# The first mixer's attention: transposes of 64-row halves, both heads in one bank

## What is computed

```python
s = jnp.einsum('nbqgrd,nbkgd->nbgrqk', qb, kw) * dh ** -0.5
p, denom, m = masked_softmax(s + bias, mask)
o = jnp.einsum('nbgrqk,nbkgd->nbqgrd', p, vw) / denom
...
o = g[..., 0:1] * o_cmp + g[..., 1:2] * o_sel + g[..., 2:3] * o_win
```

## Time and profile before

| | us |
|---|---|
| median of three runs | 1298.45 (1298.41 to 1301.5) |
| the profiled execution | 1297.85 |
| its span, first to last instruction | 1296.1 |
| the stage of the change, first turning to the output projection's first matmul | 95.27 to 141.29 |
| TensorE, VectorE, ScalarE busy in the span | 98 %, 63 %, 50 % |

### The profile page before, as it was taken

The page is one execution under the profiler, slowest core; times in us unless marked ns, Lnnn a source line. Parts: engine busy times, 40 slices in busy tenths (PEclk is TensorE's granted clock), DMA queues, the critical chain, the costliest instruction groups (busy, mean ns, idle before and its releaser), DMA issues.

```text
span 1296.1 us, 19580 instructions
## 1 busy us (share of the span) xinstructions
PE 1266.3 (98%) x7427; PEld 1058.7 (82%) x7427; DVE 812.3 (63%) x1194; ACT 641.7 (50%) x932; POOL 275.7 (21%) x362
## 2 busy tenths in 40 slices
PE   9999999999999999999999999999999999999997
PEld 7986788888799987888888788888887778888886
DVE  4568665555574476654656755656789876755554
ACT  4439554444453365543444644445544683534442
POOL 6520210000000041103000589602276210200000
PEclk9999999999999999999999999999999999999999
DMA  9960655555455645467655555654545346555651
GB/s 303 268 130 20 179 163 194 193 182 182 155 195 183 175 116 161 166 194 175 215 189 163 189 181 185 224 194 135 191 130 163 130 130 195 191 184 193 194 189 38
DMA packets 155996, 224.79 MB, mean 173 GB/s; under 512 B 13507, under 2 KB 108091, under 8 KB 155932
## 3 DMA queue, kind: packets, MB, share of 16 engines
q1 hardware_dynamic: 145248, 212.55, 51.7%
q0 software_dynamic: 10064, 10.54, 4.2%
q10 hardware_dynamic: 620, 0.83, 0.2%
HBM read 222.56 MB, written 1.25 MB: 173 GB/s over the span
## 4 chain that ended last, share of the span: by engine, by line
PE 82%; DVE 8%; ACT 4%; POOL 2%; DMA 2%; issue 2%; DVEq 0%; SPq 0%; POOLq 0%; ACTq 0%
PE bank L223 24%; PE bank L225 23%; PE bank L224 23%; PE bank L244 5%; DVE units_lo L178 2%; PE bank L232 2%; PE bank L747 1%; DMA raw_units<-in_ffn_w_up 1%; ACT arena L1584 1%; PE bank L1000 1%; DVE arena L3092 1%; PE bank L239 1%; POOL rows L1261 1%; DVE arena L3083 1%; DVE arena L2545 1%
## 5 line engine op out<-in xcount | busy, mean ns | idle before, releaser
L666 DVE TENSOR_TENSOR units_lo<-raw_units,units_hi 128x2048 fp32r<-128x2048 f32 x96 | 223.0, 2322 | 154.3 <-ACT units_hi L620 154.3
L223 PE MATMUL bank<-units_hi,turned_hi 128*128 128x512 f32 (+1 forms) x792 | 307.1, 388 | 3.0 <-DVE units_lo L178 1.3
L225 PE MATMUL bank<-units_hi,turned_lo 128*128 128x512 f32 (+1 forms) x792 | 302.1, 381 | 0.0
L224 PE MATMUL bank<-units_lo,turned_hi 128*128 128x512 f32 (+1 forms) x792 | 301.7, 381 | 0.0
L178 DVE TENSOR_TENSOR units_lo<-raw_units,units_hi 128x2048 fp32r<-128x2048 f32 (+2 forms) x101 | 228.3, 2268 | 96.0 <-ACT units_hi L170 95.6
L170 ACT ACTIVATE units_hi<-raw_units 128x2048 fp32r<-128x2048 f32 (+2 forms) x101 | 189.5, 1885 | 100.2 <-PE bank L225 76.8
L620 ACT ACTIVATE units_hi<-raw_units 128x2048 fp32r<-128x2048 f32 x96 | 183.5, 1911 | 103.9 <-PE bank L225 95.6
L223 PE MATMUL bank<-units_hi,second_hi 128*128 128x512 f32 (+1 forms) x560 | 218.7, 391 | 0.0
L225 PE MATMUL bank<-units_hi,second_lo 128*128 128x512 f32 (+1 forms) x560 | 216.5, 387 | 0.0
L224 PE MATMUL bank<-units_lo,second_hi 128*128 128x512 f32 (+1 forms) x560 | 216.4, 386 | 0.0
L223 PEld LDWEIGHTS bank<-units_hi,turned_hi 128*128 128x128 f32 x792 | 149.0, 188 | 32.8 <-DVE units_lo L178 3.0
(11 more groups left out here) (373 smaller groups left out, 1778.2 us busy)
## 6 DMA issues: line engine op xcount, KB each, us to landing
raw_units<-in_ffn_w_up SPq DMA_DIRECT2D x88, 512.0 KB, 4.7
raw_units<-in_ffn_w_in SPq DMA_DIRECT2D x88, 512.0 KB, 4.6
raw_units<-in_ffn_w_down SPq DMA_DIRECT2D x22, 1024.0 KB, 5.0
raw_units<-in_ffn_w_out SPq DMA_DIRECT2D x22, 1024.0 KB, 4.9
raw_units<-in_w_in SPq DMA_DIRECT2D x18, 1024.0 KB, 5.1
raw_units<-in_b_w_q SPq DMA_DIRECT2D x12, 1024.0 KB, 5.2
raw_units<-in_a_w_in SPq DMA_DIRECT2D x9, 1024.0 KB, 11.9
raw_units<-in_kv_w SPq DMA_DIRECT2D x6, 1024.0 KB, 5.3
```

Source lines behind the costliest of these rows:

```text
L223: pe.matmul(out, lh, rh, start=start, stop=False, skip_group_check=True)
L224: pe.matmul(out, lh, rl, start=False, stop=False, skip_group_check=True)
L225: return pe.matmul(out, ll, rh, start=False, stop=True, skip_group_check=True)
L666: dve.tensor_tensor(m.WL[:, slot(n0 + j), :], m.RAW[:, slot(n0 + j), :], m.WH[:, slot(n0 + j), :].bitcast(F32), ALU.subtract).then_inc(m.l ...
```

## The change

Each 128 by 128 transpose becomes two of 64 rows by 128 columns. The rows of the array are then split in two, as they are in the scores. Both heads' transposes of the upper 64 queries of each block go to bank 4, those of the lower 64 to bank 5: bank 4 + half holds six pieces of 64 columns, three per head. A turning now waits for both copies of the pair before it, and for each head's weighing in turn. The copies keep size, number and engine; `PT` is indexed by half instead of head, and the sums read it as pieces of 64 columns, taken from the two halves in turn. In `bias_pair_a_vector` the wait for the ring's old turning stands once ahead of both heads. The fixed distances `TURN_AFTER` and `SUM_AFTER` become the lists `TURN_AT` and `SUM_AT`, which hold the same steps, and the code is cut into two functions.

```diff
-TURN_AFTER, SUM_AFTER = 2, 3
+TURN_AT = [i + 2 for i in range(NPA)]
+SUM_AT = [t + 1 for t in TURN_AT]
...
+def wait_weighted_a(pe, m, i, par):
+    pe.wait_ge(m.s("a_weighted"), 4 * i + 2 * par + 2)
...
+def turn_pair_a_tensor(pe, m, i):
+
+    if i >= 1:
+        pe.wait_ge(m.s("a_turned_copied"), 2 * i)
+    for par in range(2):
+        wait_weighted_a(pe, m, i, par)
+        for b, at in enumerate((S, 0, P)):
+            for half in range(2):
+                rows = slice(half * DH, (half + 1) * DH)
+                to = (par * 3 + b) * DH
+                ins = pe.transpose(m.pb[4 + half][:, to:to + DH], m.A.PB[rows, i % RING_PAIRS, par, at:at + P],
+                                   m.IDENT[rows, rows])
+                if (par, b) == (1, 2):
+                    ins.then_inc(m.s("a_turned"), 1)
...
+def sum_pair_a_tensor(pe, m, i):
...
+    pe.wait_ge(m.s("a_turned_copied"), 2 * (i + 1))
+    v = (m.A.VS, m.A.VW)[br]
+    for keys, (a, b) in enumerate(((0, S), (P, S))):
+        for par in range(2):
+            g = 2 * G + par
+            blocks = slice(0, 2) if keys == 0 else slice(2, 3)
+            pt = m.A.PT[:, i % 2, :, :].rearrange("p h (x b q) -> p h x b q", x=2, b=3)[:, :, par, blocks, :]\
+                .rearrange("p h b q -> p b h q")
+            ins = mm(pe, out[par * DH:(par + 1) * DH, a:b].rearrange("p (b h q) -> p b h q", h=2, q=DH),
+                     v[:, keys, g * DH:(g + 1) * DH], pt, False, keys == 1 and br == 1)
...
-            for par in range(2):
-                pe.wait_ge(m.s("a_weighted"), 4 * i + 2 * par + 2)
-                if i >= 1:
-                    pe.wait_ge(m.s("a_turned_copied"), 2 * (i - 1) + par + 1)
-                w = m.A.PB[:, i % RING_PAIRS, par, :]
-                out = m.pb[4 + par]
-                pe.transpose(out[:, 0:P], w[:, S:S + P], m.IDENT[:, :])
-                pe.transpose(out[:, P:2 * P], w[:, 0:P], m.IDENT[:, :])
-                pe.transpose(out[:, 2 * P:3 * P], w[:, P:S], m.IDENT[:, :]).then_inc(m.s("a_turned"), 1)
...
+    if p >= RING_PAIRS:
+        dve.wait_ge(m.s("a_turned"), 2 * (p - RING_PAIRS) + 2)
     for par in range(2):
         h = 4 * (2 * G + par) + r
         dve.wait_ge(m.s("a_scored"), 2 * p + par + 1)
-        if p >= RING_PAIRS:
-            dve.wait_ge(m.s("a_turned"), 2 * (p - RING_PAIRS) + par + 1)
...
-            for par in range(2):
-                act.wait_ge(m.s("a_turned"), 2 * i + par + 1)
-                if i >= 2:
-                    act.wait_ge(m.s("a_summed"), 2 * (i - 1))
-                act.activation(m.A.PT[:, i % 2, par, :], m.pb[4 + par][:, 0:3 * P], ACT.Copy)\
-                    .then_inc(m.s("a_turned_copied"), 1)
+        for i in range(NPA):
+            if TURN_AT[i] == p:
+                for half in range(2):
+                    act.wait_ge(m.s("a_turned"), 2 * i + half + 1)
+                    if i >= 2:
+                        act.wait_ge(m.s("a_summed"), 2 * (i - 1))
+                    act.activation(m.A.PT[:, i % 2, half, :], m.pb[4 + half][:, 0:3 * P], ACT.Copy)\
+                        .then_inc(m.s("a_turned_copied"), 1)
```

More of the change, by code:

```diff
@@ L1476, in score_pair_a_tensor @@
                 ins.then_inc(m.s("a_scored"), 1)
+def wait_weighted_a(pe, m, i, par):
[14 more added lines that the diff above has]
+def sum_pair_a_tensor(pe, m, i):
+    T, G, r, br = pair_a(i)
+    out = m.pb[6 + T % 2]
+    if i == 0:
+        pe.wait_ge(m.s("cmp_ready"), TT)
+    if br == 0:
+        if T >= 2:
+            pe.wait_ge(m.s("a_out_lo"), T - 1)
+        rr = slice(32 * r, 32 * r + 32)
+        for par in range(2):
+            g = 2 * G + par
+            pe.matmul(out[par * DH:(par + 1) * DH, 0:S], m.A.VCR[rr, g, :], m.A.PCT[rr, g, :], start=True,
+                      stop=False, skip_group_check=True, tile_position=(32 * r, par * DH))
+    pe.wait_ge(m.s("a_turned_copied"), 2 * (i + 1))
+    v = (m.A.VS, m.A.VW)[br]
+    for keys, (a, b) in enumerate(((0, S), (P, S))):
+        for par in range(2):
+            g = 2 * G + par
+            blocks = slice(0, 2) if keys == 0 else slice(2, 3)
[3 more added lines that the diff above has]
+                     v[:, keys, g * DH:(g + 1) * DH], pt, False, keys == 1 and br == 1)
+            if keys == 1:
+                ins.then_inc(m.s("a_summed"), 1)
 def attend_a_tensor(pe, m):
     pe.wait_ge(m.s("a_left_out"), 5)
-    for p in range(2, NPA + SUM_AFTER):
+    for p in range(2, SUM_AT[-1] + 1):
         if p < NPA:
@@ L1485, in attend_a_tensor @@
             pe.wait_ge(m.s("a_right_out"), 5)
-        if TURN_AFTER <= p < NPA + TURN_AFTER:
-            i = p - TURN_AFTER
-            for par in range(2):
-                pe.wait_ge(m.s("a_weighted"), 4 * i + 2 * par + 2)
-                if i >= 1:
-                    pe.wait_ge(m.s("a_turned_copied"), 2 * (i - 1) + par + 1)
-                w = m.A.PB[:, i % RING_PAIRS, par, :]
-                out = m.pb[4 + par]
-                pe.transpose(out[:, 0:P], w[:, S:S + P], m.IDENT[:, :])
-                pe.transpose(out[:, P:2 * P], w[:, 0:P], m.IDENT[:, :])
-                pe.transpose(out[:, 2 * P:3 * P], w[:, P:S], m.IDENT[:, :]).then_inc(m.s("a_turned"), 1)
[L1497 to L1506, removed]
-                for par in range(2):
[L1508 to L1520, removed]
+        for i in range(NPA):
+            if TURN_AT[i] == p:
+                turn_pair_a_tensor(pe, m, i)
+        for i in range(NPA):
+            if SUM_AT[i] == p:
+                sum_pair_a_tensor(pe, m, i)
 def bias_pair_a_vector(dve, m, p):
     T, G, r, br = pair_a(p)
+    if p >= RING_PAIRS:
+        dve.wait_ge(m.s("a_turned"), 2 * (p - RING_PAIRS) + 2)
     for par in range(2):
@@ L1554, in attend_a_vector @@
 def attend_a_vector(dve, m):
-    for p in range(2, NPA + 3):
+    for p in range(2, SUM_AT[-1] + 1):
         if p < NPA:
@@ L1560, in attend_a_vector @@
         for T in range(7):
-            if LAST_PAIR[T] + 4 == p:
+            if SUM_AT[LAST_PAIR[T]] + 1 == p:
                 out_lo(dve, m, "a", T, T, m.pb[6 + T % 2][:, 0:S])
```

## The result

The changed kernel takes 1300.43 us, the median of 20 executions (1298.1 to 1306.39), against 1298.6 us for 20 executions of the kernel before beside it (1297.59 to 1301.98). The ratio is **1.0015, with a 95 % interval of 1.0008 to 1.0022**: slower by some 1.8 us. By the bound of 0.3 % that is within "same", as 94 % of the chances had it, but the time lies above the range of 1296.6 to 1300.2.

A forecast was written before the change was run, and what follows sets the result against it. TensorE's long matmuls bound the kernel; TensorE and ScalarE, waiting in turn, bound this stage's loop. Terms +0.15 - 0.33 + 0.12 = -0.06 us, set against a median of 1298.45, gave 1298.4 us, range 1296.6 to 1300.2.

The forecast's parts named there:

- the twelve transposes: Turning in the first mixer's attention: twelve of 64 rows take 0.48 us, between 0.42 and 0.52.
- pair 2: Turned early in the stage with no wait, on the path: 0.80 us becomes 0.47, so -0.33 us.
- the sums in 64-column runs: Sums reading both banks' copies in short pieces: taken as 0, at the upper end +0.4 us.
- Edits with no price: The moved bias wait on VectorE, unchanged copies and weighing order, and renamed schedule lists: claimed to cost nothing.
- The sum: All terms for the stage together: -0.06 us, with bounds of about -0.5 and +0.7 us.
- the end: From pair 14 on, ScalarE's copy waits for the last of twelve transposes: +0.12 us.
- the waiting steps: Steps where TensorE waits for ScalarE's copies before turning, five on the path: +0.03 us each, +0.15 in all.
- The clock taken for granted: Granted clock read as 1.00 throughout the stage; TensorE's copy waits growing from 4.0 to 8 or 9 us priced at nothing.
- the tour: Chain of copies, transposes, sums, scores, bias and exponentials on which the whole 6.01 us period was said to hang.
- The transposes do overlap: Rival in the turning claimed the opposite: twelve take 1.60 us, together +8.6 us, 1307 us; chance 2 %.
- ScalarE waits for no transposes in the middle periods: Rival claimed the opposite: copies stand still some 0.35 us, +5 us over 14 steps, 1303 us; chance 2 %.
- the free steps: Steps where TensorE runs straight on: worth nothing; rival: 0.25 to 0.33 us in seven, about -2 us, 1296.4; chance 5 %.

The follow-up runs named there:

- r_after: The changed kernel run once more, unchanged, on another chip: 1300.63 us, ratio to the kernel before 1.0018 (1.0006 to 1.0029).
- e1: The changed kernel with VectorE's two waits ahead of a pair's first bias in their old order: 1301.72 us, ratio to the kernel before 1.0013.
- e6: The kernel before with VectorE's two waits ordered as in the change, old turning first, once for both heads: 1299.96 us, ratio 1.0004.
- e4: The changed kernel with four matmuls nobody reads put into TensorE's first wait alone: 1300.02 us, ratio to the kernel before 1.0012.
- e5: The kernel before, with each head's turning waiting for both copies of the previous pair: 1303.3 us, ratio 1.0023.
- e8: The changed kernel, VectorE's waits in old order, six upper-half transposes behind the first copy, then six lower behind the second: 1300.55 us, ratio to before 1.0008.

## Why the prediction was wrong, step by step

**Right: the twelve transposes.** Forecast 0.48 us, measured 0.51 (120.34 to 120.85), and they start 0.06 us behind the end of the second copy instead of 0.14. Both together are 0.57 us, before 0.59: -0.02 where I had +0.03. In pair 2 the way from the first transpose to the compressed matmuls is 0.46 us in r_after (101.19 to 101.65) for 0.80, as forecast (0.47). The rule of the Trainium skill that I had weighed ("TensorE: Matmul & The Clock Gate", section "LDWEIGHTS (loading the stationary operand)") is that a load costs by its columns, however few its rows. The trace agrees for the single load: 138 ns (median) with 64 rows in r_after, 139 with 128 rows in the kernel before. The estimate of 1.28 us for twelve, which I had from it, laid them one behind the other, and that was wrong: here they overlap, and all twelve lie within 0.45 us (from 122.33 us in r_after). So the rows at L1893 that I had set against the page disagree with my sum and not with the page.

**A small term missed: the start of the turning behind scores.** Where the transposes follow scores with no wait, they now have the scores' shape: from the sums before pair 2 to its first transpose r_after takes 1.56 us (99.63 to 101.19), before 1.66 (99.62 to 101.28). That is another -0.10 at pair 2, whose whole gain is 0.44, not 0.33. That the change of shape is the reason is likely and wasn't tested alone.

**Right: the sums in 64-column runs.** From the start of sums to the start of scores it is 0.80 us in both kernels (117.44 to 118.24 before, 128.02 to 128.82 after). The upper end of +0.4 us can go.

**Wrong: "Edits with no price".** I looked at whether the moved wait could still be open, found that the old turning is long done, and priced the move at nothing. What decided was which of the two waits stands alone in VectorE's queue. Where it is the late one, the bias starts 0.11 us later: +0.11 in each of the four periods, shown by e1 and e6, and 0.57 us over the whole stage in e6. With the -0.02 of the turning that is the +0.09 by which the period grew.

**The sum.** r_after against before, both at full clock, at the compressed matmuls and measured from the scores of step 2: pair 1 -0.02; pair 2 -0.44; then +0.23 up to the first regular period (e6, the kernel before with the new order, has +0.11 over the same way; the rest wasn't taken apart); +0.09 in each of the four periods; and -0.05 over the end, where I had +0.12. Sum +0.08, forecast -0.06. That these lie within 0.14 us of each other is luck: the moved wait cost some 0.55 us (five times 0.11) that I had at nothing, and pair 2, the waiting steps and the end were each 0.1 to 0.2 us better than forecast.

**Wrong: the clock taken for granted.** I read "granted clock 1.00", forecast that TensorE's waits would double from 4.0 us to 8 or 9, which came true (7.9, and 8.8 in r_after), and called them worth nothing, as they are not on the tour. There was no rival in which they cost the clock. This is the step that made the prediction miss: some 1.3 us of the 1.55 by which the means differ, and 3.13 us in the profiled execution. A stretch of 3.4 us at the lower level made one period 0.48 us longer (6.58 for 6.10) and the two stretches of that profile together, 10.2 us, made the stage 3.13 us longer, so 0.48 is the low end; ahead of the stage 57 matmuls fit into 8 us at a clock of 0.79 and 70 at 1.00 (the first two stretches shown), which is 1.5 us lost for 3.4 us at the lower level.

The Trainium skill ("TensorE: Matmul & The Clock Gate", section "A second HAM failure mode: psum-queue depth-cycling") tells of a kernel whose clock swings between its two levels where TensorE idles briefly and often. That should have been a rival. after and e4, where the clock fell behind a wait of 1.08 us, agree with it; r_after, with the same waits, does not, and the falls of after, e1, e5 and e8 behind a first wait of 1.5 us or more are another case than that section's.

**The rivals I named.** The transposes do overlap, ScalarE waits for no transposes in the middle periods (it does so twice in r_after, 0.68 and 0.32 us, both at the end), and the free steps gained nothing, as the period of e1 is only 0.02 to 0.03 us under 6.01: none of the three happened.

## What to carry to other kernels

An engine's idle time costs nothing on the chain of waits, but TensorE's can cost its clock, as it did here in five profiles of the six with longer waits; a change that lengthens TensorE's waits needs a rival for it, with the price of a stretch at the lower level taken from the trace. Where an instruction waits for two semaphores, look in the queue's lines which of the two stands alone, and see to it that this is the one that is over early (here the one written second). When a period changes by less than the runs spread, read it from the starts of the same line in several periods, where 0.02 us shows, and undo one edit in both kernels.

## What the runs showed of the hardware

- With two waits ahead of a VectorE instruction, the one written second is an instruction of its own in the queue (L1529 and L1549, 21 ns each, in before, after, e1 and e6), and where that is the one that ends last, the next instruction starts 0.11 us later than with the waits exchanged.
- A TensorE wait of 1.08 us was followed by stretches of 3.4 us at 1.2 GHz in after and e4, and a first wait of 1.5 to 2.1 us by stretches of 3.4 us (e5) or 6.8 us (after, e1, e8). In r_after the same waits were followed by none. With the waits filled by matmuls that nobody reads the clock stayed at 1.00 in the stage, in five profiles of five.
- Two stretches at 1.2 GHz, 10.2 us together, made the stage 3.13 us longer (50.08 for 46.95 us, the same kernel).
- Twelve transposes of 64 rows take 0.51 us behind a wait, with the change to the next shape, where six of 128 rows take 0.77 (e5). A single weight load lasts the same with 64 rows as with 128 (138 and 139 ns); those of the twelve overlap.
- Transposes that had the shape of the scores ahead of them started 0.10 us earlier (1.56 for 1.66 us); that the shape is the reason wasn't tested alone.
